# Hybrid attention and recurrence trunk: the first output tile is projected in the slot of the last short tile

## The reference

```python
qa, ka, va, za, qr, fr, ir, zr = _project(_rmsnorm(x, norm_g), w_in)       # 1024 -> 8 groups of 512, 4 heads each
scores = einsum(q, k) * SCALE - slopes * |dist|, masked by chunks of 64    # two maps per head
a  = softmax(scores)[0] - lam * softmax(scores)[1]
oa = a @ v                                                                 # group A: differential attention
orec, state = gated_linear_recurrence(qr, fr, ir)                          # group B: HGRN2, state 128x128 per head
mix = concat(_rmsnorm(oa) * silu(za), _rmsnorm(orec) * silu(zr))
y = _rmsnorm(x + mix @ w_out, final_g)
```

## Time and profile before

| | |
|---|---|
| median of 3 runs | 1574.97 us (1574.3 to 1575.33) |
| profiled execution | 1575.97 us |
| its span, first to last instruction | 1574.3 us |
| mean granted TensorE clock | 0.984 |
| busy: PE, DVE, ACT, POOL | 96%, 59%, 55%, 43% |

### The profile page before, as it was taken

The page is one execution under the profiler, slowest core; times in us unless marked ns, Lnnn a source line. Parts: engine busy times, 40 slices in busy tenths (PEclk is TensorE's granted clock), DMA queues, the critical chain, the costliest instruction groups (busy, mean ns, idle before and its releaser), DMA issues.

```text
span 1574.3 us, 25558 instructions
## 1 busy us (share of the span) xinstructions
PE 1509.5 (96%) x8432; PEld 1293.2 (82%) x8432; DVE 928.2 (59%) x2087; ACT 859.2 (55%) x2325; POOL 680.6 (43%) x1407
## 2 busy tenths in 40 slices
PE   5999999998999999989999999899999999699997
PEld 4888888887888888868888888688888888588886
DVE  6676666676555566675555667665556657433232
ACT  5666666665555655565565555755565566321121
POOL 6655555535644433446454433655544433300000
PEclk9999999998999999999999999999999999799999
DMA  7242221153422222134322221314222110433431
GB/s 229 85 144 95 95 94 68 71 159 108 131 97 68 68 67 68 46 110 126 104 71 68 68 68 65 116 56 150 69 91 74 54 51 17 153 120 133 147 120 67
DMA packets 99431, 149.11 MB, mean 95 GB/s; under 512 B 10288, under 2 KB 79792, under 8 KB 90608
## 3 DMA queue, kind: packets, MB, share of 16 engines
q1 hardware_dynamic: 99312, 147.62, 28.7%
HBM read 103.03 MB, written 44.56 MB: 94 GB/s over the span
## 4 chain that ended last, share of the span: by engine, by line
PE 85%; DVE 5%; issue 3%; ACT 2%; POOL 2%; SPq 1%; DMA 1%; POOLq 0%; DVEq 0%; ACTq 0%
PE pab L570 42%; PE oar L640 7%; PE qkb L691 7%; PE pab L731 6%; PE qkb L731 6%; PE qkb L596 6%; PE tb L631 3%; DVE scores L1112 2%; PE tb L670 2%; PE tb L718 1%; SPq L305 1%; PE oar L612 1%; PE oar L609 1%; PE oar L611 1%; PE tb L536 1%
## 5 line engine op out<-in xcount | busy, mean ns | idle before, releaser
L570 PE MATMUL pab<-w_hi,xr 128*128 128x512 f32 x2176 | 785.6, 404 | 2.6 <-issue 2.4
L570 PEld LDWEIGHTS pab<-w_hi,xr 128*128 128x128 f32 x2176 | 413.9, 190 | 83.2 <-issue 3.6
L570 PE MATMUL pab<-w_lo,xr 128*128 128x512 f32 x1088 | 428.4, 394 | 0.0
L1316 POOL TENSOR_TENSOR dd<-dd 128x64 f32<-128x64 f32 x340 | 118.0, 347 | 459.3 <-DVE dd L1097 459.3
L570 PEld LDWEIGHTS pab<-w_lo,xr 128*128 128x128 f32 x1088 | 207.8, 191 | 33.2
L691 PE MATMUL qkb<-kp,q 128*128 128x512 f32 (+3 forms) x656 | 186.9, 367 | 21.6 <-DVE kp L1060 19.8
L828 ACT ACTIVATE fb<-pab 128x256 f32<-128x256 f32 x68 | 26.1, 385 | 274.4 <-PE pab L570 274.4
L1112 DVE CUSTOM_DVE_ANT_0 scores<-qkb,bias 128x512 f32<-128x512 f32 (+4 forms) x136 | 84.9, 625 | 153.1 <-PE qkb L691 153.1
L883 ACT ACTIVATE scores<-scores,nmx 128x128 f32<-128x128 f32 (+16 forms) x136 | 156.9, 1164 | 16.4 <-DVE nmx L1122 16.4
L691 PEld LDWEIGHTS qkb<-kp,q 128*128 128x128 f32 x656 | 120.6, 190 | 53.6 <-DVE kp L1060 21.2
L640 PE MATMUL oar<-vv,at 128*128 128x128 f32 x1104 | 152.5, 277 | 1.9 <-ACT at L849 1.9
(11 more groups left out here) (143 smaller groups left out, 2625.1 us busy)
## 6 DMA issues: line engine op xcount, KB each, us to landing
xr<-xs SPq DMA_DIRECT2D x51, 1024.0 KB, 5.3
xs<-xr SPq DMA_DIRECT2D x17, 1024.0 KB, 3.9
w_raw<-in_w_in SPq DMA_DIRECT2D x48, 256.0 KB, 5.8
mix<-mx SPq DMA_DIRECT2D x68, 128.0 KB, 2.2
bias<-mix SPq DMA_DIRECT2D x17, 512.0 KB, 5.0
w_raw<-in_x_prompt SPq DMA_DIRECT2D x16, 512.0 KB, 3.9
scores<-in_x_prompt SPq DMA_DIRECT2D x16, 512.0 KB, 4.2
out<-vv SPq DMA_DIRECT2D x16, 512.0 KB, 3.0
```

The lines of the kernel that those rows point to most:

```text
L570: last = mm(pab[:, b, :], x, w[:, kt, 512 * b:512 * b + 512], start=(kt == 0 and part == 0 and w is w_hi), stop=(kt == KT - 1 and part == 1))
L1316: g.tensor_tensor(o[:, :, 0, :], ref, c[:, :, 0, :], sub)
```

## The change

It has three parts.

**Order on DVE, all heads.** In slot `SAMPLE` the low parts of queries and keys come ahead of the first three splits of the second weight half. The diff of this part, with the one for ACT, which now makes all of `w_out`'s second half in the slot:

```diff
                     if t == SAMPLE:
                         split_weights(h, 1, (4, 5, 7))
-                        if h < HEADS - 1:
-                            split_weights(h, 0, (0, 1, 3))
+                    if t == SAMPLE and h == HEADS - 1:
+                        first_lo(1)
                     split_qk(h, t)
+                    if t == SAMPLE:
+                        split_weights(h, 0, (0, 1, 3))
                     biased_scores(h, t, before)
-                    if t == SAMPLE and h < HEADS - 1:
+                    if t == SAMPLE:
                         split_weights(h, 0, (4, 5, 7))
...
```

```diff
+            def first_transposes(part):
+                if part == 0:
+                    pe.wait_ge(S["mixin0"], 16)
+                    need(pe, HEADS - 1, "pb_free", NT)
+                else:
+                    pe.wait_ge(S["f0_lo"], 1)
+                for kt in range(4):
+                    d = P * (4 * part + kt)
+                    last = tr(pab[:, 1, P * kt:P * kt + P], heads_in[:, 0, d:d + P], ident[:, :])
+                last.then_inc(S[("f0_t", "fo_t")[part]], 1)
+
+            def first_project():
+                pe.wait_ge(S["fo_lo"], 1)
+                need(pe, HEADS - 1, "a_evac", NT)
+                for b, kt in [(b, kt) for b in (1, 0) for kt in range(KT)]:
+                    if b == 0 and kt == 2:
+                        epi_transposes(0, 1)
+                    if b == 0 and kt == 5:
+                        rec_scores(HEADS - 1, SAMPLE)
+                    name, n = lo_of(b, kt)
+                    need(pe, HEADS, "w_hi_ready", hi_of(b, kt))
+                    need(pe, HEADS, name, n)
+                    for part in range(2):
...
+                    if b == 1 and kt in (4, 5):
+                        qk(HEADS - 1, SAMPLE, 0, kt - 4)
+                last.then_inc(S["fo_mm"], 1)
...
-            for m in range(2):
-                qk(HEADS - 1, SAMPLE, 0, m)
-            rec_scores(HEADS - 1, SAMPLE)
-            attend(HEADS - 1, SAMPLE, False, None)
+            need(pe, HEADS - 1, "t_evac", T_USES - 1)
+            first_project()
+            attend(HEADS - 1, SAMPLE, False, None)
             need(pe, HEADS - 1, "t_evac", T_USES)
             need(pe, HEADS - 1, "qk_free", QK_USES)
-            epi_transposes(0, 0)
...
-            with pe.Fori(0, PAIRS) as i:
+            epi_transposes(1, 0)
+            epi_project(0, 1)
+            with pe.Fori(1, PAIRS) as i:
```

**Places and queue.** `heads_in` moves from `bias` to `xr` slot 2, `gains` from `kq` to the first half of `bias`, ACT's discarded squares for even tiles from `at` to its second half, and `rows_in` from `scores[:, 1]` to the second half of both maps. SP's order:

```diff
+                    if t == SAMPLE and last:
+                        need(sp, h, "proj_done", SAMPLE)
+                        need(sp, h, "mix_out0", 16 * (EVEN - 1))
+                        load_heads(0, 0)
+                        need(sp, h, "mix_out1", 16 * (ODD - 1))
+                        load_heads(0, 1)
                     if t == SAMPLE:
                         for kt in range(2):
                             raw_behind(kt)
...
+            need(sp, HEADS - 1, "mix_out1", 16 * ODD)
+            load_heads(1, 0)
+            need(sp, HEADS - 1, "at_t", NCH - 1)
             for par in range(2):
                 load_rows(0, par)
-            for par in range(2):
-                load_heads(1, par)
+            need(sp, HEADS - 1, "neg_max", NT)
+            sp.dma_start(gains[:, :], final_g...)
+            load_heads(1, 1)
+            sample_store(HEADS - 1)
```

More of the change, by code:

```diff
@@ L560, in project @@
                         transpose_recurrence(h, t, first)
+                    if b == 0 and kt == 4 and t == SAMPLE and h == HEADS - 1:
+                        first_transposes(0)
                     if b == 0 and kt == 2 and before:
@@ L618, in attend @@
                 need(pe, h, "fin_done", t)
+                if h == HEADS - 1 and t == SAMPLE:
+                    pe.wait_ge(S["fo_lo"], 2)
                 chunks = chunks_of(t)
@@ L652, in attend @@
                     last = values(c)
+                    if h == HEADS - 1 and t == SAMPLE - 1 and c == 1:
+                        first_transposes(1)
                 last.then_inc(S["pv_done"], 1)
@@ L702, in head @@
                         transpose_qk(h, t)
-            head(0, True)
-            for h in range(1, HEADS):
-                head(h, False)
-            for m in range(2):
-                qk(HEADS - 1, SAMPLE, 0, m)
-            rec_scores(HEADS - 1, SAMPLE)
-            attend(HEADS - 1, SAMPLE, False, None)
+            def first_transposes(part):
[20 more added lines that the diff above has]
+                    for part in range(2):
+                        for w in ((w_hi, w_lo) if part == 0 else (w_hi,)):
+                            last = mm(pab[:, b, :], xr[:, 0, part, kt, :], w[:, kt, 512 * b:512 * b + 512],
+                                      start=(kt == 0 and part == 0 and w is w_hi),
+                                      stop=(kt == KT - 1 and part == 1))
+                    if b == 1 and kt in (4, 5):
+                        qk(HEADS - 1, SAMPLE, 0, kt - 4)
+                last.then_inc(S["fo_mm"], 1)
             def epi_transposes(i, par):
@@ L929, in head, with first_hi @@
                         x_high(t + 2)
[L931 to L941, removed]
+            def first_hi(part):
+                act.wait_ge(S[("f0_t", "fo_t")[part]], 1)
+                F(xr[:, 0, 0, 4 * part:4 * part + 4, :].rearrange("p k c -> p (k c)"), pab[:, 1, :], ACT.Copy
+                  ).then_inc(S[("f0_hi", "fo_hi")[part]], 1)
             def epi_hi(i, par):
@@ L952, in epi_square @@
                   accum_out=tsq[:, par:par + 1]).then_inc(S["fo_sq"], 1)
-            epi_hi(0, 0)
-            with act.Fori(0, PAIRS) as i:
+            assert len(chunks_of(SAMPLE - 1)) == 4 and KT == 8
+            head(0, True)
+            for h in range(1, HEADS):
+                head(h, False)
+            softmax_exp(HEADS - 1, SAMPLE)
+            epi_hi(0, 1)
+            copy_decayed_keys(HEADS - 1, SAMPLE)
+            copy_weights(HEADS - 1, SAMPLE, (0,))
+            sum_squares(HEADS - 1, SAMPLE)
+            epi_square(0, 0)
+            epi_hi(1, 0)
+            epi_square(0, 1)
+            with act.Fori(1, PAIRS) as i:
                 epi_hi(i, 1)
@@ L1154, in head @@
                         x_low(1)
+                    if t == SAMPLE and h == HEADS - 1:
+                        first_lo(0)
                     if t == SAMPLE:
@@ L1173, in head, with first_lo @@
                         x_low(t + 2)
[L1175 to L1182, removed]
+            def first_lo(part):
+                dve.wait_ge(S[("f0_hi", "fo_hi")[part]], 1)
+                blocks = slice(4 * part, 4 * part + 4)
+                tt(xr[:, 0, 1, blocks, :].rearrange("p k c -> p (k c)"), pab[:, 1, :],
+                   xr[:, 0, 0, blocks, :].rearrange("p k c -> p (k c)").bitcast(f32), ALU.subtract
+                   ).then_inc(S[("f0_lo", "fo_lo")[part]], 1)
             def epi_lo(i, par):
@@ L1203, in epi_normalise @@
                     ALU.mult, ALU.mult).then_inc(S["fo_y"], 1)
-            epi_lo(0, 0)
-            dve.wait_ge(S["gains_in"], 32)
-            with dve.Fori(0, PAIRS) as i:
+            head(0, True)
+            for h in range(1, HEADS):
+                head(h, False)
+            combine(HEADS - 1, SAMPLE, HEADS - 1)
+            epi_lo(0, 1)
+            sum_scores(HEADS - 1, SAMPLE)
+            finish(HEADS - 1, SAMPLE)
+            assert chain[0] == PER["vec_chain"], chain[0]
+            need(dve, HEADS - 1, "v_out", 16 * NT)
+            dve.wait_ge(S["gains_in"], 32)
+            epi_add(0, 0)
+            epi_normalise(0, 0)
+            epi_lo(1, 0)
+            epi_add(0, 1)
+            epi_normalise(0, 1)
+            with dve.Fori(1, PAIRS) as i:
                 epi_lo(i, 1)
```

36 lines of the change are left out of this document (15 added, 21 removed).

## The result

| | before | after |
|---|---|---|
| median, runs beside each other | 1575.15 us (4 runs) | 1558.16 us (1556.6 to 1559.94, 4 runs) |
| profiled execution | 1575.97 us | 1557.17 us |
| its span | 1574.3 us | 1555.2 us |
| mean granted clock | 0.984 | 0.992 |

Ratio 0.9894, interval 0.9876 to 0.9911. The forecast was 23.6 us; the medians give 17.0, the two profiled executions 18.8.

What follows compares the result with a forecast made beforehand. TensorE, busy 96% of the span, was taken as the bound. Gains of 7.5 us at three head starts and 16.1 at the end sum to 23.6, giving 1551.4 us on the median's scale; range 1547 to 1560.

Steps and rivals of the forecast that it cites:

- Part 1, the order on DVE: At three head starts, splitting queries and keys before three weight splits on DVE removes PE's 6.3 us waits: 7.5 us.
- `kq` at the slow value: Head starts: `kq` slowed beside POOL's weight splits, towards 2.10 instead of 1.08 us, taken as ending at 1025.6.
- Part 2, tile 0: End of the run: tile 0 moved under the short tile starts tile 1's projection 16.1 us sooner, at full clock.
- Parts 3 and 4: Load queues on SP and the seven-turn loop: counted as 0 us and as nothing.
- rival C: Transfers for the moved tiles come late at two places: 3.0 us off, 1554.4; chance 0.07.
- rival D: At the end only tile 0's first half gives cover, as PE waits in the second: 1557; chance 0.12.
- rival E: In the loop a shared buffer lengthens the chain and PE waits every tile: 1583.4 at 2 us excess; chance 0.02.
- Rival B: Shorter stalls at the head starts and the end still let the clock fall: 16.2 us gained, 1558.8; chance 0.18.

Runs made afterwards that it cites:

- The order alone: The kernel before with only DVE's order changed at the first three heads, keys ahead of three weight splits: 1572.93 us, ratio 0.9988.
- with the clock held: The kernel before with the new DVE order at the first three heads and 15 unread matmuls per head start: 1567.58 us, ratio 0.9955.
- Scores first: The changed kernel with all six DVE splits of the second weight half behind `biased_scores`, in all heads: 1556.96 us, ratio 0.9882.

## Why the prediction was right and wrong

**The sign and the range.** Faster, with 1558.2 inside 1547 to 1560, but outside the forecast's own 1548 to 1556. 5 to 7 us of the 23.6 didn't come.

**Part 1, the order on DVE: right in mechanism, wrong in size.** The wait for `kp` went, and `rec_scores` waits for `kq`, as said. The step that failed is "PE needs 5.9 us from `rec_scores` to `attend`". This was the stretch as it ran before, at full clock, since by then PE had recovered. Now the wait lies right ahead of it, and the same stretch takes 8.35 (1023.47 to 1031.82), 2.45 more. I had named 2.2 us for half clock, which gave PE 1033.8, and then took DVE's `combine`, 1032.8, as what sets `attend`. DVE's side came as forecast: its scores are ready at 1029.66 + 0.42, 20.55 us behind the keys' transposes, forecast 20.4. But PE is last, by 1.7 us, since the clock fell at every start with the wait of 4.1. The order alone gave 1.8 us, and 7.3 with the clock held. The other 5.5 came from holding the clock; at the three starts the traces show 4.4 of them (66.73 against 62.29 us), and the last 1.1 is within the intervals. The forecast's timing of the engines was otherwise good: attend at 20.8 behind the keys' transposes with the clock held, forecast 1032.9 - (1035.42 - 22.98) = 20.5.

**`kq` at the slow value: nearly.** It ended 13.9 us behind the keys' transposes (1023.41 - 1009.53). The forecast was 13.2 (1025.6 - 1012.44), of which 0.6 was for contention. The contention cost 1.3: 0.3 is `kq` at 1.40, which the forecast had, and 1.0 `nmx`, which it hadn't. I had looked for contention only in large operations. The Trainium skill names, in "GPSIMD Engine Reference", Specifications, DVE instructions in a 2-port perf mode or with two SBUF inputs; the prediction had only the second kind. `nmx` took 1.13 beside POOL against 0.17 without it, with one SBUF input, and 1.12 with two. No run here shows in which mode the first form ran, so this doesn't speak against the page. Holding POOL back freed DVE of it and won nothing, since PE then waited for POOL and the clock fell all the same.

**Part 2, tile 0: right.** 15.4 of 16.1 in the trace, 14.2 by the medians when done alone. PE started tile 0 at 1340.19, forecast 1343.8 less the shift of 3.64, 1340.16; tile 1's projection began at 1359.72, forecast 1358.96. The forecast gaps of 1.2, 0.7, 0.8 and 1.7 us were 1.25, 0, 1.19 and 0.84, and the clock stayed at 1.00. (The prediction's offsets of 27.98 and 28.5 us stand for 327.98 and 328.5; the times that it gives behind them are right.)

**Parts 3 and 4: right.** SP issued tile 0's load at 1320.83, PE transposed it at 1326.68 without a wait (rival C is out); no long wait for `w_lo` came in the second half (rival D), and in the loop the next tile's projection starts 11.8 us behind the one before, as ever (1371.52 behind 1359.72), so rival E is out.

**Rival B** gives nearly the measured number, 1558.8, and half its story: right at the starts, where it left 1.2 us of gain per start and 1.5 came, wrong at the end, where it took 3.5 off and the clock cost nothing. The traces' 4.5 + 15.4 = 19.9 come down to the medians' 17.0 by other things: 0.9 of start-up, and 1.8 by which the medians lie closer together than the profiled pair. B's 16.2 is near that by luck; what bears B out at the starts is the windows and the runs with the clock held. Its place was even named in its own text ("at a head start PE would work only 1.4 us in the 6"), and its chance of 0.18 was too small: at the starts had shown the fall some 4 us into a stall, and I was forecasting one of 3.5 to 4.5. The rule cited there, "TensorE: Matmul & The Clock Gate", HAM oscillation (the Trainium skill), would have given the starts, and the trace agrees there (0.50 behind each wait of 4.1); at the end, with waits of 1.2, it shows 1.00.

**Which version is best.** The changed kernel with fifteen unread matmuls at each of three places: 1553.0 us, 21.7 below the kernel before and within 2 us of the forecast, which had counted on the clock. Scores first at the first three heads only, estimated at 1553.8 above, may do as well without them; it is untested, and the starts of the two differ by no more than 0.3 us each.

Open: whether scores first at three heads alone keeps what it gained at the starts, whether unread matmuls would help in other stretches (none were tried at the end, where the clock didn't fall), how long the clock stays down once it falls (at the three starts of one execution the loss differed by 1 us, without a difference in the program that I could find), and what decides which of DVE and POOL waits.

## What to carry to other kernels

When an edit turns a wait into a shorter one, price the work behind the new wait at both clock levels: the time of a stretch read from a trace in which the wait lay elsewhere doesn't carry over. Where a wait of several microseconds on TensorE can't be removed, matmuls that nobody reads, in a free bank and no longer than the wait, can be worth more than the reordering itself (5.5 against 1.8 us here). Before doing so see that TensorE is what comes last behind them; where it wasn't, they gave nothing. And look for another order first, judged place by place: scores first made the starts nearly as short without unread matmuls (3.95 us gained), and lost 3.2 at the end.

## What the runs showed of the hardware that was not expected

- A DVE instruction of two numbers per partition took 1.12 to 1.29 us beside POOL's operations at the head starts (0.40 to 1.16 at the end of the run) and 0.17 without, in both forms tried, with one SBUF input or two.
- The sharing goes either way. The same pair met as 6.41 us on DVE and 1.68 on POOL at one start, and 3.69 and 6.41 at another of the same execution. Beside DVE's gapless splits one POOL operation of 128x256 took 4.7 us longer at the second of these places than at the first.
- Behind a wait of 2.2 us for `kq` the granted clock fell at two of three starts (0.60 at the third, between 1022 and 1024), behind one of 4.1 at all three.
